# The first norm's weights come as one row and are spread by TensorE, and the first two slab units stand behind the third and fourth tile

## What the reference computes

```
z = rms_norm(x, norm_mix) @ w_in            # columns: u (256), q (768), k (192), v (192)
u, q, k, v = split(z);  q, k = rms_norm(q, q_norm), rms_norm(k, k_norm)
h = x + concat(pool_mix(u), band_attention(q, k, v)) @ w_out
y = h + (silu(n @ w_gate) * (n @ w_up)) @ w_down,   n = rms_norm(h, norm_ffn)

def rms_norm(x, g):
    return x * rsqrt(mean(x * x, axis=-1) + EPS) * g
```

## Time and profile before

| what | value |
|---|---|
| time, median of 3 runs | 2204.69 us (2202.77 to 2205.51) |
| the profiled execution: its time | 2204.6 us |
| its span, first to last instruction | 2202.8 us |
| PE busy | 2126.5 us, 97% of the span |
| DVE, ACT, POOL busy | 1326.2, 937.5, 942.1 us |
| mean granted clock of TensorE | 0.993 |

### The profile page before, as it was taken

One profiled execution on the slowest core, in us unless ns is written; L12 is line 12 of the kernel. 1 busy time (PEld: TensorE's weight loads), 2 busy tenths in 40 slices (PEclk: granted clock), 3 DMA queues, 4 the chain that ended last, 5 costly groups with the idle time before them and its releaser, 6 DMA issues.

```text
span 2202.8 us, 34411 instructions
## 1 busy us (share of the span) xinstructions
PE 2126.5 (97%) x11991; PEld 1893.1 (86%) x11991; DVE 1326.2 (60%) x2375; ACT 937.5 (43%) x2070; POOL 942.1 (43%) x626
## 2 busy tenths in 40 slices
PE   7999999999999999999999999999999899999998
PEld 6876799999999989767999999999887588899997
DVE  3558665555555555586655455554566776767665
ACT  4576442233232345764532333323467444343432
POOL 2411364455444414013643454444241356565663
PEclk9999999999999999999999999999999999999999
DMA  4101031122211233011311222211422113232321
GB/s 140 49 30 66 22 96 58 58 76 68 85 57 58 83 128 106 20 58 39 96 58 57 70 69 84 62 58 57 146 92 77 47 39 106 68 113 70 102 77 63
DMA packets 194387, 160.04 MB, mean 73 GB/s; under 512 B 7005, under 2 KB 176906, under 8 KB 194282
## 3 DMA queue, kind: packets, MB, share of 16 engines
q1 hardware_dynamic: 191326, 149.58, 22.3%
q10 hardware_dynamic: 2956, 9.08, 1.1%
HBM read 149.66 MB, written 9.07 MB: 72 GB/s over the span
## 4 chain that ended last, share of the span: by engine, by line
PE 80%; DVE 11%; ACT 5%; issue 2%; POOL 1%; DMA 1%; SPq 0%; DVEq 0%; ACTq 0%; POOLq 0%
PE ps L802 25%; PE ps L803 25%; PE ps L804 25%; DVE s_sb L1849 2%; DVE negmax L1854 2%; ACT s_sb L1384 2%; DVE h L1689 1%; PE ps L909 1%; PE ps L816 1%; DVE raw L1677 1%; PE ps L951 1%; PE ps L925 1%; DVE kt_sb L1771 1%; PE ps L980 1%; ACT pt_sb L1401 1%
## 5 line engine op out<-in xcount | busy, mean ns | idle before, releaser
L649 POOL TENSOR_TENSOR ring_lo<-raw,ring_hi 128x512 fp32r<-128x512 f32 (+1 forms) x276 | 415.3, 1514 | 404.1 <-ACT ring_hi L1250 341.9
L649 POOL TENSOR_TENSOR ring_lo<-st,ring_hi 128x512 fp32r<-128x512 f32 x198 | 266.9, 1356 | 316.5 <-ACT ring_hi L1250 316.0
L1689 DVE TENSOR_TENSOR h<-ps,h 128x512 f32<-128x512 f32 (+1 forms) x476 | 321.7, 686 | 131.9 <-PE ps L804 128.0
L802 PE MATMUL ps<-xt_hi,ring_hi 128*128 128x384 f32 (+1 forms) x1152 | 378.6, 329 | 4.8 <-DVE h L1689 2.1
L803 PE MATMUL ps<-xt_lo,ring_hi 128*128 128x384 f32 (+1 forms) x1152 | 375.0, 326 | 0.0
L804 PE MATMUL ps<-xt_hi,ring_lo 128*128 128x384 f32 (+1 forms) x1152 | 374.9, 325 | 0.0
L649 POOL TENSOR_TENSOR w_lo<-raw,w_hi 128x1024 fp32r<-128x1024 f32 x66 | 159.6, 2420 | 315.9 <-ACT w_hi L1227 315.8
L802 PE MATMUL ps<-w_hi,act_hi 128*128 128x512 f32 x704 | 279.8, 397 | 5.2 <-DVE ps L1979 2.1
L1250 ACT ACTIVATE ring_hi<-st 128x512 fp32r<-128x512 f32 x198 | 124.2, 630 | 371.8 <-DVE st L1943 276.9
L804 PE MATMUL ps<-w_hi,act_lo 128*128 128x512 f32 x704 | 279.1, 396 | 0.0
L803 PE MATMUL ps<-w_lo,act_hi 128*128 128x512 f32 x704 | 279.0, 396 | 0.0
(11 more groups left out here) (205 smaller groups left out, 4026.8 us busy)
## 6 DMA issues: line engine op xcount, KB each, us to landing
raw<-in_w_gate SPq DMA_DIRECT2D x66, 512.0 KB, 5.3
raw<-in_w_up SPq DMA_DIRECT2D x66, 512.0 KB, 4.0
raw<-in_w_down SPq DMA_DIRECT2D x66, 512.0 KB, 3.3
raw<-in_w_in SPq DMA_DIRECT2D x33, 512.0 KB, 4.0
raw<-in_w_out SPq DMA_DIRECT2D x24, 512.0 KB, 4.5
h<-in_x_prompt SPq DMA_DIRECT2D x16, 512.0 KB, 7.4
out<-h ACTq DMA_DIRECT2D x16, 512.0 KB, 2.7
xload<-in_x_prompt SPq DMA_DIRECT2D x10, 512.0 KB, 6.1
```

Of the source, the lines that this page charges most:

```text
L649: nc.gpsimd.tensor_tensor(lo, raw, hi.bitcast(F32), ALU.subtract).then_inc(done, 1)
L802: nc.tensor.matmul(out, w_hi, m_hi, start=first, stop=False, skip_group_check=onto)
L1689: nc.vector.tensor_tensor(out, ps[0:rows, bank, :], out, ALU.add).then_inc(d_free, 1)
```

## The change

Three edits. SP loads only one row of `norm_mix`, 4 KB, into partition 0 of `g_mix`, in the place of the old load but ahead of `ident`. DVE fills the first row of `headsum` with ones. PE multiplies that row of ones (one partition by 128) by the row of weights (one partition by 512), twice, so that PSUM banks 2 and 3 hold the weights on all 128 partitions, and DVE copies these 128x1024 numbers into `g_mix`. The load of the real `headsum` constant now waits until the two matmuls have run. And U0 and U1 stand behind T2 and T3, where they stood behind T3 and T5.

```diff
                 if s.p == 0:
                     load_h(s, 0)
+                    load_const(g_mix[0:1, :], norm_mix, gmix_loaded)
                     load_const(ident[:, :], c_ident, ident_loaded)
-                    load_const(g_mix[:, :], norm_mix.partition_broadcast(PART)[:, 0, :], gmix_loaded)
                     load_h(s, 1)
...
+                    sp.wait_ge(gmix_spread, 1)
                     load_const(headsum[:, :], c_ones)
...
-                    if not prev and t in (3, 5):
+                    if not prev and t in (2, 3):
 
                         pe.wait_ge(tp_free, start + 6)
-                        slab_unit(s, *FIRST_UNITS[t // 4])
+                        slab_unit(s, *FIRST_UNITS[t - 2])
...
+            pe.wait_ge(ones_ready, 1)
+            pe.wait_ge(gmix_loaded, 16)
+            for half in range(2):
+                last = nc.tensor.matmul(ps[:, 2 + half, :], headsum[0:1, :], g_mix[0:1, HALF * half:HALF * (half + 1)],
+                                        start=True, stop=True)
+            last.then_inc(gmix_spread, 1)
             pe.wait_ge(ident_loaded, 16)
...
+            nc.vector.memset(headsum[0:1, :], 1.0).then_inc(ones_ready, 1)
             nc.vector.memset(eps[:, :], EPS).then_inc(const_ready, 1)
             link(nc.vector.memset(u_tail[:, :, :, :], 0.0))
-            dve.wait_ge(gmix_loaded, 16)
+            dve.wait_ge(gmix_spread, 1)
+            nc.vector.tensor_copy(g_mix[:, :].rearrange("p (a n) -> p a n", a=2), ps[:, 2:4, :])\
+                .then_inc(gmix_ready, 1)
+            dve.wait_ge(gmix_ready, 1)
```

More of the change, by code:

```diff
@@ L349, in build @@
         gmix_loaded = sem("gmix_loaded")
+        ones_ready = sem("ones_ready")
+        gmix_spread = sem("gmix_spread")
+        gmix_ready = sem("gmix_ready")
         const_loaded = sem("const_loaded")
```

## The result

The changed kernel takes 2206.64 us (median of 20 executions, 2204.71 to 2210.02), the kernel before 2202.46 us (20 executions beside them, 2200.20 to 2205.64). The ratio is 1.0017 with a 95% interval of 1.0010 to 1.0023: slower by 3.7 us, give or take 1.4 (the two medians differ by 4.2). The forecast loss of 4.8 us lies within that interval, so the times alone do not say which of its terms failed; the traces do.

A forecast was written before the change was run, and what follows sets the result against it. PE bounds the kernel, with 80% of the chain, so a change at the start moves the point from which PE never waits. U2's delay 3.3 plus clock 1.5 makes 4.8 us; 2204.6 becomes 2209.4, range 2206.8 to 2211.6.

The forecast's parts named there:

- The forecast loss of 4.8 us: Whole kernel: U2's later start, 3.3 us, plus 1.5 us at the lower PE clock behind the idle stretch.
- The wait: PE ahead of U2: idle 2.7 us until ACT reads U0; U2 starts at 38.0, 3.3 us later.
- U0's end: First unit on PE: starts at 22.3, takes 6.1 us, partly at the lower clock, and ends at 28.4.
- the later loads: Load queue at the start: without the repeated row all later loads come 3.8 us earlier, slab 0 at 8.7.
- The spread: PE at the start: two float32 matmuls of the weight row take 3.5 us and are done at 7.7.
- POOL held DVE: Normalising of the first tiles: DVE loses 5.1 us to POOL, where it lost 4.2 us before.
- The step that failed: PE behind the idle stretch ahead of U2: clock falls for 3.4 us, costing 1.5 us.
- The rival with the clock staying up: PE ahead of U2: the stall comes but the clock stays up, 3.3 us slower, 2207.9 us; chance 0.17.
- The base: Whole kernel before the change: profiled execution 2204.6 us, median of the runs shown 2204.69, the loss added to it.
- The exclusion of DVE and POOL: Start of the kernel: DVE's normalising and POOL's splitting exclude each other, first to ask goes first; 3.27 us instead of 1.28.
- The rival that rests on its absence: Start of the kernel: POOL does not hold DVE up, U0 starts at 18.5, time 2205.6 us; chance 0.08.
- What the repeated row costs: Load queue at the start: `g_mix` held it 3.9 us by the trace, an estimated 1.5 us by the page's bandwidth.

The follow-up runs named there:

- The experiment on the order of the units: Kernel before with U0 and U1 moved behind T2 and T3, weights still loaded repeated: ratio 1.0025 (1.0015 to 1.0035) against the kernel before.
- the one on the banks: Changed kernel with U2 and U3 of the first part in PSUM banks of their own, not waiting for ACT's reads: ratio 1.0014 against the kernel before.
- with POOL held back: Kernel before with one row loaded and spread, and POOL starting slab 1 only when tile 3 is normalised: ratio 0.9987 against the kernel before.
- the spread alone: Changed kernel with U0 and U1 back behind T3 and T5, leaving the one row and its spread: ratio 0.9992 (0.9983 to 1.0002) against the kernel before.

## Why the prediction was right and where it was wrong

- **The wait was right.** The tail of tiles 4 and 5, hidden under U1 before, lies bare ahead of U2. I had U2 at 38.0, 3.3 us late; it starts at 38.04. The idle stretch was forecast at 2.7 us with ACT's read of U0 as its end, and is 2.85. The experiment on the order of the units shows whose loss it is, and the one on the banks splits the stretch in its two parts. The first matmul behind it takes 0.41 us instead of 0.18, which makes the 3.4 us at U2's start the 3.6 at the mark.
- **Several terms on the way were mis-sized and cancelled; that U0's end agrees is luck.** I took the later loads as 3.8 us earlier; slab 0's cast starts at 9.87 instead of 12.48, 2.6 earlier, and tile 1's statistics at 6.45 instead of 9.37, 2.9. The spread took 3.74 us, not 3.5, and the first normalising began at 9.44, not 9.05. I had it wait for the cast of slab 0; it came first, and the cast waited for it (1.75 us instead of 1.04). So POOL held DVE for less than I had it: 2.3 us (0.78 for the first two tiles together, 0.64 and 0.90 for the next two) and not 5.1; another 1.1 us went into waits for ACT, which I had at nothing. T2 began at 17.05, where I had 18.8. From there to the low parts of tile 2 it took 4.4 us and not 3.4: I had taken the distance from T3, but behind T2 the normalising of tile 3, held by POOL, stands ahead of those low parts. U0 started at 21.6, not 22.3. Its first matmul took 0.69 us, the clock took 5.2 us to rise (at 26.8) instead of 4.1, and U0 ended at 28.40, where I had 28.4.
- **The step that failed is the clock**: "An idle stretch of 2.7 us lies with those that lost the clock", worth 1.5 us of the 4.8. It did not fall there in this trace, nor in two of the other three with the same stretch. The stretches from which I drew the rule are themselves a matter of the execution: the one of 2.03 us near 907 us that lost the clock in the trace of before kept it in the trace after (the table at the end has all places). One trace could not show this, since in the trace of before all six stretches of 1.93 us and more lost the clock. At the one fall in four that was seen, itself a small sample, the term is worth 1.5 x 1/4 = 0.4 us, and 3.3 + 0.4 = 3.7 us; that this equals the ratio's 3.7 proves little beside an interval of 1.4 to each side. The rival with the clock staying up, 3.3 us, was given 0.17 and is what the trace shows.
- **The base failed too**: "Against the profiled execution, 2204.6", which I took as good because the median of the three runs agreed within 0.1. The median of 20 is 2202.46. Of the 2.8 us by which 2209.4 is too high, 2.1 is this. The trace of before has the clock lowered in six stretches ahead of the end, the trace after in four; both kernels' runs differ by more than 5 us among themselves. A forecast range of 2206.8 to 2211.6 took in no uncertainty of its own base.
- **The exclusion of DVE and POOL** held where it could be tested: with POOL held back the normalising took 1.28 us again. One reading of it was loose: POOL's cast from 15.89 in the earlier trace rows ends at 17.93, 0.9 us behind DVE and not just after it, so it did nearly all of its own 1.04 us once DVE was done. The rival that rests on its absence (U0 at 18.5) did not come up.
- **What the repeated row costs** depends on the execution, and I had weighed one row too far. The page "DMA: Bandwidth & Descriptors" of the Trainium skill, section Bandwidth, gives 341 GB/s for a transfer of 1 MB that GpSimd issues; by it the 512 KB, which SP issues here, are an estimated 1.5 us. Of the changed kernel's two traces the second agrees, with later loads 1.5 to 1.6 us ahead of the trace of before, and the first does not, with 2.6 to 2.9. Over all eight traces with the one row, tile 1's statistics start between 6.45 and 7.86, which is 1.5 to 2.9 us ahead of 9.37; and with the repeated row they start at 9.37 in one trace and at 10.75 in the other (the order of the units alone). None shows my 3.8 against the trace of before.

## What to carry to other kernels

Moving matrix work forward in an in-order queue moves everything behind it back: before doing it, ask what chain on the other engines starts only from the work that is pushed back, and what covers that chain's tail afterwards. Ahead of the first matmul, look at who holds whom between VectorE and GpSimd; a wait that puts GpSimd's two-input work under something else was worth 1.3 us at the mark for one line. Take the base of a forecast from many runs, or carry its spread into the range. And a rule on the clock that one trace bears out six times of six can still be a matter of the execution: a price of it needs the same place in several traces.

## What the hardware showed unasked

An idle TensorE in the first 20 us is not free: with its gaps filled by transposes that nobody reads, the clock was up for good from 10.5 us instead of 22.4 in the same kernel without them, and the mark stood 2.0 us earlier. In the spread alone the clock was up for a while before U0: T0 and T1 take 3.25 us there and 3.85 in the changed kernel, which puts the rise near 13.5, and it was low again from 16.9 until 23.7, past U0's start:

```profile
13.50:16.90 3.40, 1.11 (x10) 0.87 (x9) 2.49 (x4) 3.34 (x8) 3.40 (x2) 1.00 0.81 225
16.90:23.70 6.80, 3.85 (x17) 3.45 (x16) 6.71 (x7) 4.62 (x12) 2.60 (x2) 0.50 0.88 243
```

The spread matmuls ahead of it are not shown to be the cause: the changed kernel has the same ones, and with twice as many T0 and T1 took 3.85 us too.

The changed kernel, in its two traces, kept the clock behind an idle stretch of 2.03 us and lost it behind one of 2.03 us at the same place of its program. The windows just behind the stretch, of the first execution:

```profile
912.80:916.30 3.50, 3.50 (x19) 3.23 (x19) 2.04 (x6) 2.32 (x5) 0.00 (x0) 1.00 0.00 0
```

And of the second:

```profile
913.70:917.10 3.40, 3.40 (x12) 3.40 (x11) 2.68 (x6) 1.58 (x4) 0.00 (x0) 0.50 0.00 0
```

The same idle stretches of PE stand in all ten traces of this case, the two kernels and the eight runs. Behind them the granted clock was 0.50 or stayed at 1.00:

| idle stretch | its place | clock fell | clock stayed up |
|---|---|---|---|
| 1.85 to 1.88 us | near 800 and near 1730 | 0 | 20 |
| 1.92 to 1.94 us | near 1605 | 8 | 2 |
| 2.01 to 2.03 us | near 910 | 5 | 5 |
| 2.07 to 2.11 us | near 1575 | 6 | 4 |
| 2.69 to 2.70 us | near 1790 | 1 | 9 |
| 2.71 to 2.73 us | near 135 | 8 | 2 |
| 2.85 or 2.86 us | ahead of U2, in four traces | 1 | 3 |
| 6.97 to 6.99 us | near 1755 | 10 | 0 |

Ahead of U2 stretches of 1.90 and 2.54 us stood once each as well, and the clock stayed up. So between 1.9 and 2.9 us the length alone does not tell: 2.7 us near 1790 kept the clock nine times of ten, and 2.7 us near 135 lost it eight times of ten. What decides was not tried and stays open.
